# A hybrid attention trunk step on one core: a tile's rows ahead of due weight loads on SyncE, and one more mixer A head transposed on TensorE

## The chip, the cores and the metric
One core of a Trainium2 chip runs one program. The metric is the device time in microseconds (us) of one execution; the time before is the median of three runs. TensorE, VectorE (DVE), ScalarE (ACT), GpSimd (POOL) and SyncE (SP) run their own instruction streams and meet at semaphores. SP computes nothing here: it waits and issues DMAs.

## What is computed
The kernel is one layer of a diffusion trunk in float32, on 128 context tokens and 512 latent tokens (5 tiles of 128 tokens) of width 2048:

```
h = rms_norm(x) * g * (1 + scale) + shift       # scale, shift, gate = silu(cond) @ w_ada + b_ada
z = h @ w_in                                    # 2048 -> 6656 columns, the larger product
mixer A, 8 heads:  p = softmax(q1 k1) - lam * softmax(q2 k2);  o = rms_norm(p @ v) * silu(gate)
mixer B, 8 heads over 2 key heads: p = softmax(q k);           o = (p @ v) * silu(gate)
y = rms_norm(x + gate * (concat(o) @ w_out))
```

The context tile (tile 0) attends to its own 128 keys. Each latent tile (tiles 1 to 4) attends to 512 latent and 256 cached keys, 768 in all. Rotary positions, the key and value states and the cached context are part of it and are not touched here.

## The kernel before, in words
The large products are cut into 17 iterations (`it`) of 512 output columns: `it` 0 is the keys and values of mixer B, 1 to 4 are mixer B's query and gate columns (kind "G", two heads each), 5 to 12 are mixer A's heads (kind "D", one head each), 13 to 16 are the output projection. Each has 16 steps (`s`), one for each 128 rows of the weights. A step multiplies one 128x512 weight slice with the five token tiles, each as three matmuls (L775 to L777) on operands that were split into a high and a low part. `q` counts steps: q = 16 it + s from `it` 2 on. (The first two iterations are cut into pieces that take turns.)

The attention of group `a = it - 1` is laid between the products of iteration `it`, by a table of steps (`STEPS`, `STEPS_D`). For tile t, "S" is the scores, "T" the transposition of the probabilities and "V" the product with the values. S is at steps 4, 5, 7, 9, 11 for tiles 0 to 4, T at 6, 8, 10, 12, 14, V at 7, 9, 11, 13, 15. An S piece of kind "G" claims four banks one after another, one of kind "D" three, out of a ring of three PSUM banks (`claim`, L763); V claims the next bank. A bank is free when ACT has copied it out (`scores_out`, L1199). In G, the fourth score bank is the first one again; in D, the bank of V(t=0) at step 7 is the first bank of the scores of tile 2 at the same step.

**Weights.** They come in pairs of slices (pair j holds steps 2j and 2j+1; here numbered within an iteration, so pair 5 holds steps 10 and 11). SP loads a pair with two DMAs of 256 KB (`load_w`, L639) into one of two raw buffers, after VectorE has split the pair that was there: pair j waits until slice 2j-3 is split (`w_lo_done` 2j-2). At the head of its step, ACT rounds the slice of three steps on into `w_hi` (`split_w`, L1138, `W_AHEAD = 3`), and it waits for the whole pair there; VectorE then makes `w_lo` (L1541). So slice 10 is rounded at step 7.

**Probabilities.** For every latent tile, ACT copies the scores to `s_sb`, VectorE takes the maximum (`score_max`, L1640), ACT the two exponentials (`exps`, L1239), one step after S. In D, VectorE then combines the two maps into one (`combine`, L1648, `p_ready`). Transposing is done in one of two ways. `by_blocks(a, t)` is true for latent tiles of groups 1 to 11: SP writes the rows to HBM (`p_spill`, 384 KB for a map, two maps in G, one in D), waits until they have landed, and reads them back by 32-row blocks with four DMAs (`p_pair` in G, `p_block` in D; `move_blocks`, L711); VectorE transposes 32x32 blocks (`turn_blocks`, L1664), and in G ACT and VectorE split the result again (`blocks_hi`, `blocks_lo`). Otherwise TensorE transposes six 128x128 blocks into two banks (`step_t`, L933), and ACT copies them out (`pt_his`, L1248). Before, only group 12, mixer A's last head, does that for its latent tiles.

**SP's order.** SP goes through the steps. At each q whose step before held an S by blocks (steps 6, 8, 10, 12) it first issues the pairs up to q // 2 + 3 that are not yet issued, each with its wait, and then calls `move_blocks`: wait for the exponentials (G) or `p_ready` (D), spill, wait for the landing, read the blocks. At step 6 the pairs 2 to 6 are thus issued ahead of tile 1's rows; at steps 8, 10 and 12 it is one pair each.

During iteration 12 (group 11) GpSimd also reads the first output rows back from HBM (`load_row`, L2057), ACT and VectorE split them (`row_hi`, L1313).

Of the kernel before, what the change touches and what calls it, by code (L numbers as in the profile page):

```python
# [36 lines left out]
KV_IT = 0  # L37
G_IT = 1
D_IT = G_IT + H_B // 2
OUT_IT = D_IT + H_A  # L40
# [27 lines left out]
ORDER = [(it, s) for it, k0, k1 in SEGMENTS for s in range(k0, k1)]  # L68
# [57 lines left out]

def by_blocks(a, t):

    return t > 0 and KV_IT < a < OUT_IT - 1


def group_kind(a):
    return "KV" if a == KV_IT else "G" if a < D_IT else "D"
# [6 lines left out]
def steps_at(it, s):  # L140

    out = []
    if it > OUT_IT:
        return out
    if it == KV_IT + 1:
        return [("QK", KV_IT, 0)] if s == KV_QK_STEP else []
    for kind, t in (LAST_STEPS if it == OUT_IT else STEPS_D if group_kind(it - 1) == "D" else STEPS).get(s, []):
        a = it - 1
        if kind == "O":
            a, t = a + t, 0  # L150
        if not 0 <= a < OUT_IT or (group_kind(a) == "KV" and kind != "QK"):
            continue
        if kind == "O" and group_kind(a) == "G":
            continue
        out.append((kind, a, t))
        if kind == "V" and group_kind(a) == "G":
            out.append(("GT", a, t))
    return out
# [135 lines left out]
def build(nc, x_prompt, x_sample, cache_diff_k, cache_diff_v, cache_gqa_k, cache_gqa_v, c, c_ctx, w_ada,  # L294
# [120 lines left out]
    with ExitStack() as ctx:  # L415
# [48 lines left out]
        def wait_full(eng, n):  # L464

            b, i = PLACE[n]
            eng.wait_ge(bank_full[b], i + 1)
# [42 lines left out]
        def n_step(a, t):  # L510

            return TILES * (a - 1) + t
# [34 lines left out]
        def t_parts(a, t):  # L547
# [7 lines left out]
            return [(n + 2 * c + j // 4, c, j, m, 0, True) for c in hs for j, m in ((0, 4), (4, 2))]  # L555

        TURNED = [(a, t) for a in range(OUT_IT) for t in range(TILES) if by_blocks(a, t)]

        def p_count(a, t):

            return sum(heads(of) for of, u in TURNED[:TURNED.index((a, t)) + 1] if u % 2 == t % 2)

        def turns_until(a, t):

            return sum(heads(of) for of, _ in TURNED[:TURNED.index((a, t)) + 1])
# [62 lines left out]
        def ada_place(m):  # L628

            c_ = max(c for c in range(BLOCKS) if ADA_LOAD0[c] <= m)  # L630
            return c_, m - ADA_LOAD0[c_]

        def ada_slot(m):

            c_, _ = ada_place(m)
            ks = 8 // ADA_TILES[c_]
            return ada_raw[:, m % ADA_RING, :].rearrange("p (k u n) -> p k u n", k=ks, u=2), ks

        def load_w(eng, j):  # L639
            it, s = ORDER[2 * j]  # L640
            if j >= RAW_RING:

                eng.wait_ge(w_lo_done, 2 * (j - RAW_RING) + 2)
            dst = w_raw[:, j % RAW_RING]
            landed = (raw_first if RAW_RING <= j < EARLY_PAIRS else raw_in)[j % RAW_RING]
            if D_IT <= it < OUT_IT:
                for u in range(2):
                    eng.dma_start(dst[:, u, :].rearrange("p (s c) -> p s c", s=4),
                                  wa_v[it - D_IT, :, s + u]).then_inc(landed, 16)
                return  # L650
            if it == KV_IT:
                for u in range(2):
                    eng.dma_start(dst[:, u, :], w_v[:, s + u, KB0:KB0 + NCOL]).then_inc(landed, 16)
            elif it < D_IT:
                for u, c0 in enumerate((QB0, GB0)):
                    c0 += 2 * DH * (it - G_IT)
                    eng.dma_start(dst[:, :, 2 * DH * u:2 * DH * (u + 1)],
                                  w_v[:, s:s + 2, c0:c0 + 2 * DH]).then_inc(landed, 16)
            else:
                c0 = NCOL * (it - OUT_IT)  # L660
                for u in range(2):
                    eng.dma_start(dst[:, u, :], wo_v[:, MIX[s + u], c0:c0 + NCOL]).then_inc(landed, 16)
# [16 lines left out]
        @block.sync  # L679
        def _(sp):  # L680
            def load_ada(n):

                m = n - ADA_RING
                if m >= 0:
                    c_, e = ada_place(m)
                    if e == ADA_LOADS[c_] - 1:
                        wait_full(sp, TURN[("ADA", c_)])
                    else:
                        sp.wait_ge(ada_used, m - c_ + 1)
                c_, e = ada_place(n)  # L690
                dst, ks = ada_slot(n)
                w = P * ADA_TILES[c_]
                for u in range(2):
                    c0 = D_MODEL * u + P * ADA_FIRST[c_]
                    sp.dma_start(dst[:, :, u, :], ada_p[:, ks * e:ks * (e + 1), c0:c0 + w]  # L695
                                 ).then_inc(ada_in[n % ADA_RING], 16)

            def load_x(t):
                src = x_prompt[0] if t == 0 else xs_v[:, t - 1, :]
                sp.dma_start(x_sb[:, t, :], src).then_inc(x_in[t], 16)  # L700

            for t in FIRST_TILES:
                load_x(t)
            for n in range(ADA_LOADS[0]):
                load_ada(n)
            for j, t in enumerate(LATER_TILES):
                load_w(sp, j)
                load_x(t)
            for n in range(ADA_LOADS[0], sum(ADA_LOADS)):
                load_ada(n)  # L710
            def move_blocks(a, t):  # L711

                b, n = t % 2, TURNED.index((a, t))
                if group_kind(a) == "G":
                    for c_ in range(2):
                        sp.wait_ge(exp_done, 2 * n_step(a, t) + 1 + c_)
                        sp.dma_start(p_spill[b, c_], s_sb[:, b, c_, :]).then_inc(p_out[b], 16)
                else:
                    sp.wait_ge(p_ready, n_step(a, t) + 1)
                    sp.dma_start(p_spill[b, 0], s_sb[:, b, 0, :]).then_inc(p_out[b], 16)  # L720
                if n:
                    sp.wait_ge(p_turned, turns_until(*TURNED[n - 1]))
                if (a, t) == (D_IT, 1):
                    wait_full(sp, TURN[("V", D_IT - 1, TILES - 1)])
                sp.wait_ge(p_out[b], 16 * p_count(a, t))
                for i in range(QUAD):
                    rows = slice(SUB * i, SUB * (i + 1))
                    if group_kind(a) == "G":
                        src = p_spill[b].rearrange("c (j b) (i n) -> i b (c j) n", j=QUAD, i=QUAD)[i]
                        dst = p_pair[rows, :, :, :].rearrange("b c j n -> b (c j) n")  # L730
                    else:
                        src = p_spill[b, 0].rearrange("(j b) (i n) -> i b j n", j=QUAD, i=QUAD)[i]
                        dst = p_block[rows, :, :]
                    sp.dma_start(dst, src).then_inc(p_in, 16)

            j = EARLY_PAIRS
            for q in range(OPEN, len(ORDER)):
                moves = [(a, t) for kind, a, t in steps_at(*ORDER[q - 1]) if kind == "S" and by_blocks(a, t)]
                if moves:
                    while j <= min(q // 2 + 3, len(ORDER) // 2 - 1):  # L740
                        load_w(sp, j)
                        j += 1
                for a, t in moves:
                    move_blocks(a, t)
            for j in range(j, ITS * KT // 2):
                load_w(sp, j)
            for t in range(TILES - 1):
                dst = y_prompt[0] if t == 0 else y_sample[0, P * (t - 1):P * t, :]
                sp.wait_ge(y_left, t + 1)
                sp.dma_start(dst[:, 0:Y_LEFT], y_sb[:, t, 0:Y_LEFT]).then_inc(y_out, 16)  # L750
                sp.wait_ge(y_right, t + 1)
                sp.dma_start(dst[:, Y_LEFT:], y_sb[:, t, Y_LEFT:]).then_inc(y_out, 16)
            dst = y_sample[0, P * (LAT - 1):P * LAT, :]
            sp.wait_ge(y_right, TILES)
            sp.dma_start(dst[:, 2 * NCOL:3 * NCOL], y_sb[:, TILES - 1, 2 * NCOL:3 * NCOL]).then_inc(y_out, 16)
            sp.wait_ge(y_left, TILES)
            sp.dma_start(dst[:, 0:NCOL], y_sb[:, TILES - 1, 0:NCOL]).then_inc(y_out, 16)
            sp.wait_ge(y_out, 32 * (TILES + 1))
# [1480 lines left out]
```

## Time and profile before
| what | us |
|---|---|
| median of 3 runs (lowest, highest) | 1241.37 (1240.06, 1243.22) |
| the profiled execution | 1243.36 |
| its span, first to last instruction | 1241.6 |
| TensorE matmul busy | 1187.5 (96% of the span) |
| VectorE busy | 848.7 (68%) |
| ScalarE busy | 589.0 (47%) |
| GpSimd busy | 258.6 (21%) |

The span is shorter than the execution's time, since that has a start and an end in which no instruction of the program runs. "Idle" in a row is the time in which the engine had nothing running before that instruction; behind it stands what ended it. The mean granted TensorE clock over the span is 0.996 of full speed.

### The profile page before, as it was taken

The page shows a single profiled execution, that of the slowest core. Times are in us where ns is not written, and L with a number is a line of the kernel's source. Part 1 is how long each engine was busy: PE and PEld are TensorE (multiplying, and loading weights), DVE is VectorE, ACT ScalarE, POOL GpSimd, SP SyncE. Part 2 cuts the span into 40 slices and gives each one's busy share as a digit, 9 for nine tenths or more (in the row PEclk, how much of TensorE's full clock was granted, in tenths as well). Part 3 has the DMA queues.
Part 4 walks back from the last instruction along what each step waited for, and adds up shares of the span by engine and source line. Part 5 has one row for each costly group of instructions (what it writes and reads, how often), then busy time and mean ns, then how long its engine had stood idle before and what let it go on. Part 6 is the DMA issues. An engine that isn't in the chain of part 4 may idle for free.

```text
span 1241.6 us, 16426 instructions
## 1 busy us (share of the span) xinstructions
PE 1187.5 (96%) x5891; PEld 957.4 (77%) x5891; DVE 848.7 (68%) x1270; ACT 589.0 (47%) x1236; POOL 258.6 (21%) x439
## 2 busy tenths in 40 slices
PE   5899999999999999999999999999999799999996
PEld 3455788777787778888878888888878678888785
DVE  4455488768687786767667675857667574879674
ACT  5422235635556455555555464555555655312123
POOL 1211033012030030222222322222223312210111
PEclk9999999999999999999999999999999999999999
DMA  9999232635536355343444444453435523756644
GB/s 352 371 379 358 85 111 94 195 85 175 153 103 178 107 181 163 112 146 113 136 126 121 138 134 125 123 151 96 151 113 172 172 68 110 263 180 218 187 137 177
DMA packets 172658, 203.63 MB, mean 164 GB/s; under 512 B 12080, under 2 KB 131536, under 8 KB 171808
## 3 DMA queue, kind: packets, MB, share of 16 engines
q1 hardware_dynamic: 158704, 156.80, 39.9%
q0 software_dynamic: 13424, 45.20, 11.2%
q8 instruction: 47, 0.77, 0.3%
q10 hardware_dynamic: 448, 0.57, 0.1%
q14 instruction: 35, 0.29, 0.1%
HBM read 167.77 MB, written 34.75 MB: 163 GB/s over the span
## 4 chain that ended last, share of the span: by engine, by line
PE 81%; DMA 5%; DVE 4%; SPq 3%; ACT 3%; issue 3%; POOL 1%; DVEq 0%; ACTq 0%; POOLq 0%
PE z_ps L775 22%; PE z_ps L777 22%; PE z_ps L776 22%; PE ring L959 4%; SPq L695 2%; PE ring L866 2%; PE ring L963 2%; PE ring L801 2%; PE ring L900 2%; PE ring L899 2%; DMA p_pair<-p_spill 1%; DMA p_spill<-s_sb 1%; ACT s_sb L1245 1%; DMA ada_raw<-in_w_ada_dram 1%; PE ring L966 1%
## 5 line engine op out<-in xcount | busy, mean ns | idle before, releaser
L775 PE MATMUL z_ps<-w_hi,xt_hi 128*128 128x512 f32 x1350 | 544.4, 403 | 3.4 <-issue 1.1
L777 PE MATMUL z_ps<-w_hi,xt_lo 128*128 128x512 f32 x1350 | 527.7, 391 | 0.0
L776 PE MATMUL z_ps<-w_lo,xt_hi 128*128 128x512 f32 x1350 | 527.2, 391 | 0.0
L1082 ACT ACTIVATE w_hi<-w_raw 128x512 fp32r<-128x512 f32 x270 | 169.5, 629 | 340.2 <-PE z_ps L777 315.1
L775 PEld LDWEIGHTS z_ps<-w_hi,xt_hi 128*128 128x128 f32 x1350 | 254.4, 188 | 73.8 <-issue 27.2
L777 PEld LDWEIGHTS z_ps<-w_hi,xt_lo 128*128 128x128 f32 x1350 | 253.7, 188 | 54.8
L1544 DVE TENSOR_TENSOR w_lo<-w_raw,w_hi 128x512 fp32r<-128x512 f32 x270 | 195.9, 729 | 144.2 <-ACT w_hi L1082 143.4
L776 PEld LDWEIGHTS z_ps<-w_lo,xt_hi 128*128 128x128 f32 x1350 | 254.7, 189 | 43.4
L1645 DVE TENSOR_REDUCE small<-s_sb 128x2 f32<-128x1536 f32 (+1 forms) x60 | 88.0, 1467 | 22.2 <-ACT s_sb L1082 22.2
L1245 ACT ACTIVATE s_sb<-s_sb,small 128x768 f32<-128x768 f32 (+1 forms) x120 | 98.0, 820 | 3.0 <-DVE small L1645 2.7
L2028 POOL TENSOR_TENSOR sg<-sg,zs 128x128 f32<-128x128 f32 (+1 forms) x60 | 39.4, 656 | 266.1 <-DVE sg L1614 265.4
L1082 ACT ACTIVATE o_sum<-ring 128x128 f32<-128x128 f32 (+1 forms) x60 | 18.8, 313 | 153.5 <-PE ring L959 102.0
L1818 DVE SCALAR_TENSOR_TENSOR gate_acc<-gate_raw,cs,gate_acc 128x512 f32<-128x512 f32 x120 | 84.6, 746 | 3.1 <-DMA gate_raw<-in_w_ada_dram 0.6
L1614 DVE RECIPROCAL sg<-sg 128x128 f32<-128x128 f32 (+1 forms) x60 | 72.5, 1208 | 0.0
L1082 ACT ACTIVATE s_sb<-ring 128x512 f32<-128x512 f32 (+2 forms) x140 | 57.6, 473 | 11.8 <-PE ring L900 10.9
L959 PEld LDWEIGHTS ring<-v_f,pt_f 128*128 128x128 f32 x400 | 50.7, 193 | 15.1 <-issue 12.6
L959 PE MATMUL ring<-v_f,pt_f 128*128 128x128 f32 x400 | 52.2, 278 | 9.5 <-issue 6.5
L1082 ACT ACTIVATE s_sb<-ring,stat 128x512 f32<-128x512 f32 (+1 forms) x72 | 37.7, 554 | 20.2 <-PE ring L777 19.9
L899 PE MATMUL ring<-k_hi,q_hi 128*128 128x256 f32 (+2 forms) x144 | 45.0, 325 | 0.0
L963 PE MATMUL ring<-pt,v_hl 128*128 128x512 f32 x100 | 36.4, 401 | 8.8 <-issue 8.8
L900 PE MATMUL ring<-k_hi,q_lo 128*128 128x256 f32 (+2 forms) x144 | 44.0, 329 | 0.0
L1671 DVE STREAM_TRANSPOSE pt_f<-p_block 128x768 f32<-128x768 f32 x28 | 27.3, 976 | 23.3 <-DMA p_block<-p_spill 23.3
(200 smaller groups left out, 1302.0 us busy)
## 6 DMA issues: line engine op xcount, KB each, us to landing
w_raw<-in_w_in_dram SPq DMA_DIRECT2D x188, 256.0 KB, 3.2
ada_raw<-in_w_ada_dram SPq DMA_DIRECT2D x64, 512.0 KB, 11.7
p_spill<-s_sb SPq DMA_DIRECT2D x60, 384.0 KB, 3.6
w_raw<-in_w_out_dram SPq DMA_DIRECT2D x64, 256.0 KB, 3.7
p_pair<-p_spill SPq DMA_DIRECT2D x64, 192.0 KB, 3.6
gate_raw<-in_w_ada_dram POOLq DMA_DIRECT2D x12, 1024.0 KB, 7.8
p_block<-p_spill SPq DMA_DIRECT2D x112, 96.0 KB, 2.2
w_raw<-in_w_in_dram POOLq DMA_DIRECT2D x20, 256.0 KB, 6.3
```

Source lines behind the costliest of these rows:

```text
L775: pe.matmul(out, hi_l, hi_r, start=start, stop=False)
L776: pe.matmul(out, hi_l, lo_r, start=False, stop=False)
L777: return pe.matmul(out, lo_l, hi_r, start=False, stop=stop)
L899: pe.matmul(out, q_hi[c_][:, q0:q0 + P], keys, start=start, stop=False, skip_group_check=True)
L900: ins = pe.matmul(out, q_lo[c_][:, q0:q0 + P], keys, start=False, stop=True, skip_group_check=True)
L959: ins = pe.matmul(bank[:, 0:DH], pt_f[:, keys], v_f[:, vt, :], start=(j == 0), stop=last)
L1082: return act.activation(out, in_, ACT.Copy, **kw)
L1245: act.activation(row, row, ACT.Exp, bias=nmax[:, t, c_:c_ + 1], accum_out=den[:, t, c_:c_ + 1]).then_inc(exp_done, 1)
L1544: dve.tensor_tensor(lo, w_raw[:, kg // 2 % RAW_RING, kg % 2, :], hi.bitcast(F32), ALU.subtract).then_inc(w_lo_done, 1)
L1614: dve.reciprocal(sg[:, t, 0:w], sg[:, t, 0:w]).then_inc(g_inv, 1)
L1645: dve.tensor_reduce(nmax[:, t, :], s_sb[:, t % 2, :, 0:(NKEY if t else P)], AX_X, ALU.max, negate=True).then_inc(max_ready, 1)
L1818: ins = dve.scalar_tensor_tensor(acc[:, r, :], src, weight, acc[:, r, :], ALU.mult, ALU.add)
```

## The change
Two edits. `by_blocks` is now false for group 11 too, so the latent tiles of mixer A's last two heads are transposed on TensorE. And `move_blocks` is cut in two: `move_rows` waits for the rows and spills them, `move_blocks` waits for the landing and reads the blocks. At a step with moves SP now issues the pairs up to (q + 3) // 2, then the rows, then the pairs up to q // 2 + 3, then the block reads. At step 6 that puts pairs 2 to 4 ahead of tile 1's rows and pairs 5 and 6 behind them; at steps 8, 10 and 12 the first part is empty and the one pair goes behind the rows.

```diff
 def by_blocks(a, t):
-    return t > 0 and KV_IT < a < OUT_IT - 1
+    return t > 0 and KV_IT < a < OUT_IT - 2
...
-            def move_blocks(a, t):
-                b, n = t % 2, TURNED.index((a, t))
+            def move_rows(a, t):
+                b = t % 2
                 if group_kind(a) == "G":
                     for c_ in range(2):
                         sp.wait_ge(exp_done, 2 * n_step(a, t) + 1 + c_)
                         sp.dma_start(p_spill[b, c_], s_sb[:, b, c_, :]).then_inc(p_out[b], 16)
                 else:
                     sp.wait_ge(p_ready, n_step(a, t) + 1)
                     sp.dma_start(p_spill[b, 0], s_sb[:, b, 0, :]).then_inc(p_out[b], 16)
+
+            def move_blocks(a, t):
+                b, n = t % 2, TURNED.index((a, t))
                 if n:
                     sp.wait_ge(p_turned, turns_until(*TURNED[n - 1]))
...
                 moves = [(a, t) for kind, a, t in steps_at(*ORDER[q - 1]) if kind == "S" and by_blocks(a, t)]
+                if moves:
+                    while j <= min((q + 3) // 2, len(ORDER) // 2 - 1):
+                        load_w(sp, j)
+                        j += 1
+                for a, t in moves:
+                    move_rows(a, t)
                 if moves:
                     while j <= min(q // 2 + 3, len(ORDER) // 2 - 1):
                         load_w(sp, j)
                         j += 1
                 for a, t in moves:
                     move_blocks(a, t)
```

## Rows read from the trace of the kernel before
**Rows 1.** The page, part 1: busy us (share), instructions.
```profile
PE 1187.5 (96%) x5891; PEld 957.4 (77%) x5891; DVE 848.7 (68%) x1270; ACT 589.0 (47%) x1236; POOL 258.6 (21%) x439
```
**Rows 2.** Waits of TensorE, whole span: us in total, times, longest.
```profile
PE ring L963 <- issue: 8.8, 8, 2.5
PE ring L959 <- issue: 6.5, 4, 3.5
...
PE ring L775 <- ACT s_sb L1082: 2.5, 4, 0.9
```
**Rows 3.** Chain that ended last, 200 to 230 us: start, us, what.
```profile
210.20 1.96 ACT s_sb L1245 x4
...
212.24 4.15 DMA p_spill<-s_sb
```
**Rows 4.** TensorE's timeline, G group 1, idle before in brackets: tile 2's fourth score bank, tile 1's V.
```profile
215.76 0.28 PE L775 MATMUL ring<-k_hi,q_hi 128*128 128x256 f32 x1
...
228.28 0.47 PE L963 MATMUL ring<-pt,v_hl 128*128 128x512 f32 x1 [0.67 <-issue]
```
**Rows 5.** TensorE's timeline, G group 1: tile 4's V.
```profile
260.58 0.47 PE L963 MATMUL ring<-pt,v_hl 128*128 128x512 f32 x1 [2.46 <-issue]
```
**Rows 6.** SyncE's timeline, G group 1, tile 4: start, us, issues.
```profile
244.07 0.91 SPq L657 DMA_DIRECT2D w_raw<-in_w_in_dram  x2
245.03 0.94 SPq L717 DMA_DIRECT2D p_spill<-s_sb  x2
249.85 1.80 SPq L734 DMA_DIRECT2D p_pair<-p_spill  x4
```
**Rows 7.** DMA issues at 526.6 and 523.5 us: KB each, median us to landing.
```profile
p_spill<-s_sb SPq DMA_DIRECT2D x1, 384.0 KB, 2.3
...
w_raw<-in_w_in_dram SPq DMA_DIRECT2D x2, 256.0 KB, 3.1
```
**Rows 8.** SyncE's timeline in D group 5: pair 5, then tile 1's rows.
```profile
514.90 0.93 SPq L648 DMA_DIRECT2D w_raw<-in_w_in_dram  x2
...
526.60 0.34 SPq L720 DMA_DIRECT2D p_spill<-s_sb  x1
```
**Rows 9.** ScalarE's timeline in D group 5, step 7: slice 10's rounding.
```profile
525.73 0.63 ACT L1082 ACTIVATE w_hi<-w_raw 128x512 fp32r<-128x512 f32 x1 [0.72 <-PE z_ps L777]
```
**Rows 10.** ScalarE's timeline in G group 1, step 7.
```profile
212.24 0.63 ACT L1082 ACTIVATE w_hi<-w_raw 128x512 fp32r<-128x512 f32 x1
213.54 1.05 ACT L1082 ACTIVATE s_sb<-ring,stat 128x512 f32<-128x512 f32 x2 [0.67 <-PE ring L777]
```
**Rows 11.** TensorE's timeline in D group 5: V of tile 0.
```profile
530.27 0.38 PE L959 MATMUL ring<-v_f,pt_f 128*128 128x128 f32 x2
```
**Rows 12.** VectorE's timeline in G group 1, steps 7 and 8.
```profile
214.46 1.74 DVE L1614 RECIPROCAL sg<-sg 128x256 f32<-128x256 f32 x1
216.92 1.75 DVE L1645 TENSOR_REDUCE small<-s_sb 128x2 f32<-128x1536 f32 x1 [0.72 <-ACT s_sb L1082]
...
222.42 1.84 DVE L1671 STREAM_TRANSPOSE pt_raw<-p_pair 128x768 f32<-128x768 f32 x2 [2.03 <-DMA p_pair<-p_spill]
```
**Rows 13.** TensorE's timeline in group 12: four transposes of tile 1's probabilities.
```profile
1025.83 0.60 PE L866 MATMUL ring<-ident,s_sb 128*128 128x128 f32 x4
```
**Rows 14.** TensorE's timeline in group 11: V of tiles 2 and 4.
```profile
967.33 0.91 PE L959 MATMUL ring<-v_f,pt_f 128*128 128x128 f32 x6 [2.68 <-ACT s_sb L1082]
...
985.78 2.19 PE L959 MATMUL ring<-v_f,pt_f 128*128 128x128 f32 x12 [3.52 <-issue]
```
**Rows 15.** ScalarE's and VectorE's timelines in group 11: row operand, tile 4's blocks.
```profile
962.07 0.74 ACT L1082 ACTIVATE xt_hi<-row_st 128x640 fp32r<-128x640 f32 x1 [5.26 <-DMA row_st<-o_spill]
...
984.70 0.98 DVE L1671 STREAM_TRANSPOSE pt_f<-p_block 128x768 f32<-128x768 f32 x1 [3.65 <-DMA p_block<-p_spill]
```
**Rows 16.** Stages: stretch, us, busy us of each engine, granted clock, DMA share, GB/s.
```profile
985.00:990.00 5.00, 4.22 (x18) 3.77 (x19) 2.25 (x4) 1.37 (x4) 0.87 (x3) 0.66 0.29 105
...
1000.00:1055.00 55.00, 54.62 (x293) 46.37 (x294) 32.10 (x52) 31.84 (x74) 11.85 (x25) 1.00 0.28 91
```

## The prediction, made before the changed kernel ran
> **What bounds the kernel now.** I read the page's busy shares first. TensorE's matmuls cover 1187.5 us of the span, 96% [rows 1], so a change pays only where it shortens TensorE's stream or takes a wait out of it. Next the waits of TensorE [rows 2]: behind the opening, they are few and sit in the attention. Eight waits before V of kind G (L963) sum to 8.8 us, four before a score bank of G (L775) to 2.5, and four before V of kind D (L959) to 6.5. The chain of waits tells what lies behind those of G: the exponentials end at 212.16, the second spill (issued at 212.24) lands 4.15 us later, then come the reads and the transposition [rows 3]. V of tile 1 waits 0.67 in this group [rows 4], 2.7 over four groups, so tile 4's V holds the other 6.1 of the 8.8; its longest is 2.46 [rows 5].
>
> **The change part by part.** *Tile 4 in G, rows first.* SP issues a pair of weights in 0.91, then two spills in 0.94, and the reads start at 249.85 [rows 6]. The second spill's issue starts near 245.5, so it takes 4.3 to land, as in the chain (4.15). A spill with no pair just ahead lands in 2.3 [rows 7]. The new order thus brings the landing forward by 1.9 to 2.0, and by up to 0.4 more where the pair's issue held up the spill. The pair now goes out 0.9 after the second spill's issue began and lands 3.1 after its own issue [rows 7], while the reads are issued 2.3 after the spill and need about as long again to arrive: I charge them 0 to 0.5. Behind the blocks stand ACT and VectorE, both waiting. So 2.46 shrinks to about 0.5, and the other three, which share the 3.6 that is left of the 6.1 (1.2 each, less than what the landing gains), go. Gain 5.6; bounds 3 and 6.1.
>
> *Pair 5 in D.* This is what the change costs. In D group 5 the pair was issued at 514.90, and tile 1's rows, when VectorE had them ready, at 526.60 [rows 8]. Pair 5 now stands behind these rows. But it holds slice 10, which ACT rounds at the head of step 7, at 525.73 [rows 9]: before the rows are even ready. New times: spill issued 526.60 to 526.94, the pair's two DMAs from 526.98 (0.93 for both, the second near 527.4), landing of the second 3.1 to 3.3 after that, 530.6. ACT stands until then, 4.9 late. It rounds (0.63), then copies the first score bank of tile 2 (half of 1.05 [rows 10]): 531.85. That bank is the one that V of tile 0 claims, at 530.27 [rows 11]. With a hand-over of 0.1, V starts at 531.95: TensorE waits 1.7. Nothing covers it, as TensorE takes its instructions in order. What is queued behind ACT's wait is the copies, tile 0's output and the exponentials of tile 2; VectorE waits behind it for w_lo, GpSimd behind both. They lag TensorE by some 2 to 3 us at step 8, and are busy 47% and 68% [rows 1], so they regain it before tile 4: each V stands four steps behind its S. Below, a landing 2.4 after the pair's issue (nearly the lone spill's) gives 0.9; above, 4.15 (the landing behind other traffic) gives 2.7. I take 1.7, as the 3.1 is of the same DMA. Six D groups (5 to 10) are left with rows by blocks: 6 x 1.7 = +10.2; bounds +5 and +16. Tile 2 to 4's pairs (7, 8, 9) are wanted three steps after they go out, 10 us and more, against some 4 us of delay: nothing.
>
> *Tile 1 in G.* The same happens. The exponentials end at 212.16, the second spill goes out from 212.24, pair 5 from 212.7, and lands near 216.3; ACT wanted it at 212.24 [rows 10]. It rounds until 216.95 and frees the first score bank at 217.5; TensorE wanted that bank for tile 2's fourth part at 215.76 [rows 4]: a new wait of 1.8. In exchange tile 1's blocks come sooner. The spill lands at 214.6 instead of 216.4, but pairs 5 and 6 (1 MB) are now ahead of the reads, so the blocks are there near 221.5. VectorE is not ready for them: w_lo of slice 10 at 217.65, a reciprocal of 1.74, the maximum of 1.75 to 221.1 (it was 216.92 to 218.67), then the work that stood between the maximum and the transposes less its idle time: 222.42 - 2.03 - 218.67 = 1.7 [rows 12]. The transposes start at 222.9, 0.5 later than before, and V of tile 1 at 228.8 instead of 228.28. So the old waits (2.7 and 2.5 us in four groups) are swapped for new ones of the same size, plus 0.5 in this group, and a bit more where the old wait was shorter: I take 0.7 on average, +2.9. Bounds: -3 (VectorE gets its work in between) and +7 (nothing of the old waits goes).
>
> *Group 11 on TensorE.* Removed: the spill, four reads and a transpose on VectorE for each of four tiles. Added: 24 transposes on TensorE, two more banks and two copies on ACT for each tile. Four transposes take 0.60 with the tail of the last (about 0.27): 0.11 each [rows 13], six with the return to the product 0.8, four tiles 3.2. What goes: V of tile 4 waits 3.52 [rows 14] for blocks that land at 984.7 [rows 15]; and behind this wait the granted clock is 0.66 over 5 us [rows 16], a loss of 1.7. V of tile 2 waits 2.68 [rows 14] for a score copy that ACT makes late, since it stood 5.26 for a row operand [rows 15]. That stays, as the row's DMA does not belong to the change; but the transposes of tiles 1 and 2 (1.6) fall into this wait and cost nothing. ACT's extra copies, 1 us for each tile, are paid by what it no longer waits for that row, whose DMA shares its engines with fewer others; 0.4 may be over. Sum: -3.5 - 1.7 + 1.6 - 0.4 = -4.0. Bounds: +0.5 (the rows set the pace in this group whatever else goes) and -7.
>
> The clock is the place where the Trainium skill speaks against this edit. In this trace the stretch from 1000 to 1055, in which the last head's transposes lie, has a granted clock of 1.00 [rows 16], the 2.4 GHz level, and four transposes take 0.60 [rows 13]. The Trainium skill (TensorE: Matmul & The Clock Gate, Part 4: PE-mode transpose) says that transposes do not count as busy time for the clock, and gives about 275 ns for one in a kernel. By the Trainium skill's figure, an estimate, 24 would cost 6.6 us instead of 3.2, and the sum below would be 3.4 higher. The trace does not agree with it here.
>
> *Sum.* -5.6 + 10.2 + 2.9 - 4.0 = +3.5. On the profiled execution's 1243.4 that is 1246.9. The median of the runs shown is 2.0 lower (1241.4), and the same sum on it gives 1244.9, which I forecast. All terms come from one execution; their differences hold for the others too.
>
> **The rivals.**
> *The late pair stays hidden (faster).* If ACT's wait for pair 5 did not reach TensorE, the D groups would cost nothing, and in G the old waits of tile 1 would go as well: -5.6 - 5.2 + 0.5 - 4.0 = -14.3, 1227. For it: ACT and VectorE have idle time. Against it: V of tile 0 comes 3.7 after the spill's issue, and the pair can't be landed, rounded and one bank copied in that time unless its landing takes 1.6 or less. Half way between, a pair that costs 0.9 in each D group gives -1.3: 1240.
> *Reads stuck behind the pairs (much slower).* At tile 4 the reads now follow a pair on the same queue. If they land 1.5 later for it (I allow 0.5), V of tile 4 waits in every group: the G gain shrinks by 3, each D group adds 1, and the lag of ACT is not regained: +3.5 + 9 = 1254. It decides from a read landing over 1.5 behind what it was.
> *Group 11 gains nothing.* The row operands (5.26) set the pace, and copies on ACT come on top: 0 instead of -4.0, 1249.
> *The transposes slow TensorE's clock.* At the 0.66 of [rows 16] over the 3.2 us of transposes and as long again, 6.4 / 0.66 - 6.4 = +3.3: 1248. Against it stands the 1.00 of the last head's stretch. (The Trainium skill's section named above has transposes count for nothing with the clock.)
>
> **How the numbers follow.** The main case has 0.50 (own range 1241 to 1248.5, from the D term between 6.5 and 14), the hidden pair 0.08, the half hidden one 0.14, the stuck reads 0.12, group 11 without gain 0.13, the slow clock 0.03. A measurement tells 0.3% (3.7 us) from no change here, so slower begins at 1245.1. Slower: half of the main case, the stuck reads, group 11 and the clock, less a little for their low ends, 0.49. Same: the rest of the main case and most of the half hidden one, 0.39. Faster: 0.12. The range leaves out the fully hidden pair and most of the stuck reads: 1238 to 1251.
>
> **What would show it.** In the changed trace: in each D group ACT waits 4 to 5 us before the rounding of slice 10 (step 7) with w_raw's DMA as the releaser, and TensorE 1.5 to 2 before V of tile 0, in six places; in G the same wait of ACT, and about 1.8 before the last score bank of tile 2. G's spills land in about 2.3 instead of 4.15, and tile 4's V waits under 0.6. Group 11 has 24 more transposes, no wait of 3.5 before its last V and a clock of 1.00 there. I am wrong if TensorE has no wait at step 7, or if tile 4's waits in G stay.

## The result, and the profile after

| | us |
|---|---|
| before, median of 4 runs beside it (lowest, highest) | 1241.93 (1240.06, 1243.22) |
| after, median of 4 runs | 1266.27 (1262.65, 1267.34) |
| ratio, 95% interval | 1.0192 [1.0167, 1.0217] |
| span before, after | 1241.6, 1265.5 |
| forecast (range) | 1244.9 (1238 to 1251) |

The kernel became 24 us slower, and the forecast had said 3.5. To see where, I cut both spans at the first product of iterations 2, 6, 12 and 13, so that the first stretch holds groups 1 to 4 (G), the second groups 5 to 10 (D), the third group 11. Stages of the kernel before; the columns are the stretch, its length, busy us (instructions) of PE, PEld, DVE, ACT, POOL, the granted clock, DMA share and GB/s:

```profile
183.91:498.19 314.28, 302.99 (x1466) 250.13 (x1465) 237.00 (x311) 164.71 (x314) 49.73 (x42) 1.00 0.48 142
498.19:911.59 413.40, 410.28 (x2062) 345.23 (x2061) 281.64 (x431) 225.19 (x528) 104.94 (x205) 1.00 0.43 129
911.59:990.86 79.27, 71.64 (x362) 58.92 (x360) 52.99 (x82) 44.69 (x101) 27.09 (x51) 0.98 0.51 156
```

The same stages after:

```profile
184.43:497.57 313.14, 303.54 (x1466) 251.64 (x1465) 236.85 (x311) 164.12 (x314) 48.45 (x42) 0.99 0.50 142
497.57:941.95 444.38, 418.35 (x2063) 349.62 (x2061) 281.01 (x431) 221.09 (x528) 98.41 (x205) 0.98 0.43 120
941.95:1015.94 73.99, 72.57 (x385) 59.95 (x384) 49.68 (x78) 47.17 (x105) 26.27 (x48) 1.00 0.42 124
```

Length less TensorE's busy time is its idle time. G: -1.1. D: +31.0, of which idle 3.1 to 26.0 is +22.9 and busy +8.1, with the same matmuls (one record apart). Group 11: -5.3. The rest of the span: -0.7. Together +23.9, the difference of the spans.

TensorE's waits after (in us: total, times, longest) answer to [rows 2]; L969 is V of D, L973 V of G, L785 a product or score matmul, L1092 a copy on ACT:

```profile
PE ring L969 <- issue: 13.7, 6, 3.1
PE ring L969 <- ACT s_sb L1092: 12.3, 6, 2.1
...
PE ring L785 <- ACT s_sb L1092: 8.6, 4, 2.2
...
PE ring L973 <- issue: 1.0, 3, 0.6
```

The six of 12.3 are V of tile 0 at step 7 in D. The four of 8.6 are tile 2's fourth score bank in G. The six of 13.7 are V of tile 4 in D, one for each group. Before, there were 3.0 us (6.5 less group 11's 3.5 in [rows 2, 14]), in three of the six groups.

Group 5 after, step by step. SyncE's timeline, to be held against [rows 8]:

```profile
525.99 0.34 SPq L720 DMA_DIRECT2D p_spill<-s_sb  x1
526.37 2.30 SPq L648 DMA_DIRECT2D w_raw<-in_w_in_dram  x4
528.83 1.82 SPq L738 DMA_DIRECT2D p_block<-p_spill  x4
```

ScalarE's timeline there (against [rows 9]); the wait is in brackets:

```profile
530.51 0.63 ACT L1092 ACTIVATE w_hi<-w_raw 128x512 fp32r<-128x512 f32 x1 [6.12 <-DMA w_raw<-in_w_in_dram]
531.05 1.06 ACT L1092 ACTIVATE s_sb<-ring 128x512 f32<-128x512 f32 x2
```

VectorE's, which waits behind ScalarE for the same slice:

```profile
531.17 0.69 DVE L1554 TENSOR_TENSOR w_lo<-w_raw,w_hi 128x512 fp32r<-128x512 f32 x1 [4.35 <-ACT w_hi L1092]
531.78 0.94 DVE L1624 RECIPROCAL sg<-sg 128x128 f32<-128x128 f32 x1
532.79 1.75 DVE L1655 TENSOR_REDUCE small<-s_sb 128x2 f32<-128x1536 f32 x1
...
535.06 0.97 DVE L1681 STREAM_TRANSPOSE pt_f<-p_block 128x768 f32<-128x768 f32 x1
```

TensorE's, V of tile 0 at step 7 (against [rows 11]) and V of tile 4 at step 15:

```profile
531.77 0.46 PE L969 MATMUL ring<-v_f,pt_f 128*128 128x128 f32 x2 [1.97 <-ACT s_sb L1092]
...
567.31 0.91 PE L969 MATMUL ring<-v_f,pt_f 128*128 128x128 f32 x6 [3.04 <-issue]
```

Ahead of that last wait, VectorE waits twice for blocks, tile 3's and tile 4's:

```profile
555.43 0.98 DVE L1681 STREAM_TRANSPOSE pt_f<-p_block 128x768 f32<-128x768 f32 x1 [2.47 <-DMA p_block<-p_spill]
...
556.80 1.02 DVE L1672 SCALAR_TENSOR_TENSOR s_sb<-s_sb,small 128x768 f32<-128x768 f32 x1
...
566.23 0.98 DVE L1681 STREAM_TRANSPOSE pt_f<-p_block 128x768 f32<-128x768 f32 x1 [5.11 <-DMA p_block<-p_spill]
```

Most of the +8.1 of busy time sits behind some of the waits. TensorE's timeline in group 6:

```profile
605.59 0.46 PE L969 MATMUL ring<-v_f,pt_f 128*128 128x128 f32 x2 [2.04 <-ACT s_sb L1092]
...
607.87 0.63 PE L785 MATMUL z_ps<-w_hi,xt_hi 128*128 128x512 f32 x1
608.29 0.63 PE L786 MATMUL z_ps<-w_lo,xt_hi 128*128 128x512 f32 x1
...
610.46 0.39 PE L786 MATMUL z_ps<-w_lo,xt_hi 128*128 128x512 f32 x1
610.69 0.39 PE L787 MATMUL z_ps<-w_hi,xt_lo 128*128 128x512 f32 x1
```

From 606.6 to 610.0 the starts of equal matmuls are 0.43 apart, later 0.23: the clock went to its 1.2 GHz level after the wait and came back to 2.4. The stages around it (columns as above):

```profile
594.00:603.00 9.00, 9.00 (x44) 7.44 (x43) 4.32 (x6) 2.74 (x6) 3.06 (x6) 1.00 0.39 110
603.00:613.00 10.00, 7.96 (x32) 6.20 (x31) 7.12 (x9) 6.45 (x16) 1.06 (x3) 0.83 0.49 121
```

D has four such stretches at the lower level and no more; before it had none:

```profile
606.56:609.97 3.41, 3.41 (x9) 2.64 (x8) 3.24 (x3) 2.17 (x5) 0.92 (x2) 0.50 0.26 56
715.79:719.20 3.41, 3.41 (x11) 2.80 (x11) 0.90 (x2) 1.49 (x5) 1.54 (x4) 0.50 0.02 5
790.88:794.29 3.41, 3.41 (x14) 3.02 (x13) 1.45 (x3) 1.14 (x4) 0.62 (x2) 0.50 0.00 0
865.98:869.39 3.41, 3.41 (x12) 2.83 (x11) 1.00 (x2) 1.37 (x4) 1.34 (x4) 0.50 0.00 0
```

Each begins 0.6 to 1.2 us after a wait has ended: the first after a wait of 2.04 at step 7, the others after waits of 2.94, 3.15 and 2.30 at tile 4. The other eight of the twelve waits, the 3.04 above among them, had none behind them. Half of 4 x 3.41 is 6.8 of the 8.1. The other 1.3 is about what the profile adds for the waits themselves (an estimate): the last matmul ahead of a wait is shown with its whole 0.39, where the next would have begun after 0.23, and there are nine more waits.

In G, SyncE at tile 4 of group 1, against [rows 6]:

```profile
245.59 1.26 SPq L717 DMA_DIRECT2D p_spill<-s_sb  x2
246.89 1.07 SPq L657 DMA_DIRECT2D w_raw<-in_w_in_dram  x2
249.37 1.81 SPq L738 DMA_DIRECT2D p_pair<-p_spill  x4
```

The second spill (246.50) lands at 249.30, in 2.8 instead of 4.3, and tile 4's V no longer waits in any of the four groups.

### The profile page after: what moved, and what is told of

Same layout as the page of the kernel before. It is cut to its first block, busy times and chain, and to the rows that moved or that the text cites. A ratio compares the mean times of both kernels' runs of the same rounds, so it can differ in the third digit from the quotient of the medians.

```text
span 1265.5 us, 16454 instructions
## 1 busy us (share of the span) xinstructions
PE 1200.0 (95%) x5915; PEld 966.3 (76%) x5915; DVE 844.6 (67%) x1266; ACT 586.7 (46%) x1240; POOL 250.9 (20%) x439
## 4 chain that ended last, share of the span: by engine, by line
PE 79%; DMA 6%; DVE 5%; ACT 4%; issue 3%; SPq 2%; POOL 1%; DVEq 0%; ACTq 0%; POOLq 0%
PE z_ps L785 21%; PE z_ps L787 21%; PE z_ps L786 21%; PE ring L969 3%; DMA w_raw<-in_w_in_dram 3%; PE ring L876 2%; PE ring L811 2%; ACT s_sb L1255 2%; PE ring L973 2%; PE ring L910 1%; PE ring L909 1%; DMA row_st<-o_spill 1%; DMA ada_raw<-in_w_ada_dram 1%; SPq L695 1%; PE ring L976 1%
## 5 line engine op out<-in xcount | busy, mean ns | idle before, releaser
L785 PE MATMUL z_ps<-w_hi,xt_hi 128*128 128x512 f32 x1350 | 548.0, 406 | 2.6 <-issue 1.1
L1092 ACT ACTIVATE w_hi<-w_raw 128x512 fp32r<-128x512 f32 x270 | 169.6, 629 | 386.3 <-PE z_ps L787 302.1
L785 PEld LDWEIGHTS z_ps<-w_hi,xt_hi 128*128 128x128 f32 x1350 | 256.1, 190 | 73.1 <-issue 27.2
L2038 POOL TENSOR_TENSOR sg<-sg,zs 128x128 f32<-128x128 f32 (+1 forms) x60 | 35.7, 595 | 295.5 <-DVE sg L1624 295.5
L1092 ACT ACTIVATE o_sum<-ring 128x128 f32<-128x128 f32 (+1 forms) x60 | 18.9, 316 | 146.5 <-PE ring L969 95.5
L969 PE MATMUL ring<-v_f,pt_f 128*128 128x128 f32 x400 | 53.4, 282 | 26.0 <-issue 13.7
L969 PEld LDWEIGHTS ring<-v_f,pt_f 128*128 128x128 f32 x400 | 50.8, 195 | 33.2 <-issue 31.1
L1092 ACT ACTIVATE s_sb<-ring 128x512 f32<-128x512 f32 (+2 forms) x136 | 55.1, 476 | 3.6 <-PE ring L910 3.4
L1681 DVE STREAM_TRANSPOSE pt_f<-p_block 128x768 f32<-128x768 f32 x24 | 23.4, 976 | 41.6 <-DMA p_block<-p_spill 41.5
L1092 ACT ACTIVATE s_sb<-ring,stat 128x512 f32<-128x512 f32 (+1 forms) x72 | 37.3, 554 | 15.2 <-PE ring L787 14.9
L1972 POOL TENSOR_SCALAR small<-small 128x1 f32<-128x1 f32 x40 | 8.0, 199 | 153.9 <-ACT sq_o L1298 152.9
```

What stands on the lines that cost most here:

```text
L785: pe.matmul(out, hi_l, hi_r, start=start, stop=False)
L969: ins = pe.matmul(bank[:, 0:DH], pt_f[:, keys], v_f[:, vt, :], start=(j == 0), stop=last)
L1092: return act.activation(out, in_, ACT.Copy, **kw)
```

## The experiments

Each kernel below stands beside runs of the kernel before on one chip, but not all kernels ran on the same chip; the stretches are from one profiled execution of each. L(G), L(D) and L(11) are the lengths of the three stretches, D's waits are those of the waits view, (the bank that ACT frees late, at step 7; V of tile 4), and D's busy time is that of the stages. Each ratio is to the runs of before beside that kernel, whose medians are 1241.1 to 1243.0.

```
kernel                    median (runs)  ratio [95%]             L(G)   L(D)   L(11)  D: ACT's bank, tile 4, busy
before                    1241.9 (4)                             314.3  413.4  79.3    -     3.0   410.3
group 11 only             1234.6 (4)     0.9950 [.9932, .9967]   313.5  412.6  73.3    -     2.4   410.2
order only                1274.9 (4)     1.0273 [1.0256, 1.0290] 313.7  437.6  85.6   12.4  10.1   415.1
changed kernel            1266.3 (4)     1.0192 [1.0167, 1.0217] 313.1  444.4  74.0   12.3  13.7   418.4
pair 5 ahead              1231.6 (4)     0.9914 [.9895, .9932]   302.0  421.0  73.6    -     8.8   412.1
late pair only            1262.6 (4)     1.0170 [1.0152, 1.0188] 319.4  435.8  74.3   12.6   6.8   416.4
rows ahead in G only      1225.6 (6)     0.9858 [.9837, .9879]   303.4  413.6  73.8    -     3.3   410.3
 + D tile 4               1227.7 (5)     0.9882 [.9863, .9901]   302.3  415.7  73.8    -     5.1   410.7
 + D tiles 1 to 3         1228.7 (6)     0.9894 [.9874, .9914]   301.9  416.9  73.9    -     6.3   410.6
 + group 10 on TensorE    1227.1 (5)     0.9876 [.9857, .9894]   302.1  415.4  74.1    -     2.3   413.1
 + late pair 5, 6 behind  1245.7 (10)    1.0028 [1.0011, 1.0044] 302.2  435.8  73.3   12.8   6.6   416.5
changed + copies first    1271.8 (4)     1.0243 [1.0219, 1.0267] 315.0  447.9  73.6    1.4  25.1   421.4
late pair + copies first  1275.2 (4)     1.0276 [1.0249, 1.0303] 322.6  440.1  74.0    1.9  18.4   419.7
G only + copies first     1236.3 (6)     0.9951 [.9936, .9967]   311.7  414.2  73.6    -     4.1   410.2
```

("Order only" runs the same code in D as the changed kernel, and its D is 6.8 shorter: 3.6 of it at tile 4's waits, and 3.3 in busy time, as it has two stretches at the low clock where the changed kernel has four. So with the late pair a stage of D is reproduced only to some 7 us, where it is 412.6 to 413.6 in the three kernels that keep the order of before in D. With copies first, the waits for ACT's bank, 1.4 and 1.9, are at step 9, and those put down to tile 4 hold one or three small ones of other tiles.)

**Group 11 only**, to the kernel before:
```diff
-    return t > 0 and KV_IT < a < OUT_IT - 1
+    return t > 0 and KV_IT < a < OUT_IT - 2
```


> Only group 11's latent tiles go to TensorE; SP's order is that of the kernel before. In the changed kernel, iteration 12 takes 74.0 us from its first product to the next iteration's, against 79.3 before. Both theories below say nothing of it; if the edits add up, this kernel is 4 to 6 us faster than before (1236 to 1238) with iteration 12 at 74. If the gain in iteration 12 hangs on the other edit, it is under 2 us.

Measured: 0.9950 [0.9932, 0.9967], 1234.6, a little under the expected 1236 to 1238; group 11 is shorter by 5.9. The edit is a gain by itself.

**Order only**: the changed kernel with `OUT_IT - 1` again.

> Only SP's order is changed; group 11 is still transposed by blocks. If the edits add up: the 24.3 us of the whole change plus the 5.3 that group 11 gives, about +30 us (1271 to 1273). Group 11 now also has a late pair 5 and rows ahead, so some 2 to 6 us more are possible (up to 1278).

Measured: 1.0273, 1274.9, inside what was expected. The order carries the whole loss, and without the other edit group 11 suffers from it too: 85.6 against 79.3.

**Pair 5 ahead of tile 1's rows** (pair 6 still behind them, and one pair behind the rows at steps 8, 10 and 12):
```diff
-                    while j <= min((q + 3) // 2, len(ORDER) // 2 - 1):
+                    while j <= min((q + 4) // 2, len(ORDER) // 2 - 1):
```


> The changed kernel with one number different: pair 5 goes ahead of tile 1's rows at step 6 ((q + 4) // 2 instead of (q + 3) // 2); at steps 8, 10 and 12 the rows stay ahead. Theory (late pair): all D waits follow from slice 10 coming late; the six waits of 2.2 before V of tile 0 go, tile 4's waits in D fall from 14.7 to about 4, the slow clock behind them goes, and G gets both its gains: 1225 to 1230. Rival (reads stuck): tile 4's waits in D come from the reads behind a pair at steps 10 and 12; they stay at 12 to 15 us with part of the slow clock, and the time is about 1240 to 1246.

**Late pair only**: step 6 as in the change, steps 8, 10 and 12 as before.
```diff
-                    while j <= min((q + 3) // 2, len(ORDER) // 2 - 1):
+                    while j <= min((q + 3) // 2 if q % KT == 6 else q // 2 + 3, len(ORDER) // 2 - 1):
```


> The changed kernel with the late pair alone: pairs 5 and 6 behind tile 1's rows at step 6, but at steps 8, 10 and 12 the pair ahead of the rows as before. Theory (late pair): tile 4's waits in D stay at 10 us or more, as ACT's and VectorE's lag reaches tile 4 by itself; in G tile 4's waits (6 us) come back: 1264 to 1272. Rival (reads stuck): tile 4's waits in D fall to 4 or less; with G's 6 us back the time is 1252 to 1258.

Measured: with the pair in time, no wait at step 7 is left, and the kernel is faster than before, 0.9914 [0.9895, 0.9932]. But neither pair of expectations holds at tile 4. With the pair in time its waits are 8.8, between the theory's 4 and the rival's 12 to 15, and 1231.6 is above the theory's range; with the late pair alone they are 6.8, between the rival's 4 or less and the theory's 10 or more. Both edits reach tile 4. With "group 11 only" and the changed kernel these two make a square of D: 412.6 (neither), 421.0 (rows ahead), 435.8 (late pair), 444.4 (both). The late pair costs 23, the rows ahead 8 to 9, and the two add up to the 444.4, but not to the 437.6 of "order only": the sum is known no better than D is reproduced. TensorE's waits with the late pair alone:

```profile
PE ring L969 <- ACT s_sb L1092: 12.6, 6, 2.3
PE ring L785 <- ACT s_sb L1092: 8.6, 4, 2.4
PE ring L969 <- issue: 6.8, 4, 3.3
PE ring L973 <- issue: 5.3, 4, 2.4
```

Its +23.2 in D are 12.6 at step 7, 4.4 more at tile 4 (6.8 against 2.4) and 6.2 of busy time, with three stretches of 3.41 at the low clock (5.1). The +8.4 of the rows ahead are 6.4 at tile 4 (8.8 against 2.4) and 2.0 of busy time, with one such stretch (1.7).

**Rows ahead in G only**: pair 5 in time, D in the old order.
```diff
-                    while j <= min((q + 3) // 2, len(ORDER) // 2 - 1):
+                    while j <= min((q + 4) // 2 if group_kind(moves[0][0]) == "G" else q // 2 + 3, len(ORDER) // 2 - 1):
```


> The changed kernel, but with pair 5 ahead of tile 1's rows in G, and with the order of before at every tile in D (all due pairs ahead of the rows); group 11 on TensorE as changed. Theory (the three parts add up: G gains 12 where pair 5 is not late, D loses nothing with the old order, group 11 gains 6): groups 1 to 4 take 302, groups 5 to 10 take 413, the time is 1223 to 1225 against 1241. The rival, that G's gain has a price later (VectorE or the queues carry a lag from G into D), keeps D at 418 or more and the time at 1228 or more.

Measured: 1225.6, just above the expected range and the fastest of all; D is 413.6, so nothing is paid back later. Its waits:

```profile
PE ring L969 <- issue: 3.3, 4, 1.5
PE ring L973 <- issue: 1.9, 4, 0.7
```

On top of it, the same bound with `or moves[0][1] == 4` behind the G (tile 4 of D too), or with `or moves[0][1] < 4` (tiles 1 to 3 of D):

> As the kernel with rows ahead in G only, but in D tile 4's rows too go ahead of the one pair due at step 12; tiles 1 to 3 of D keep the order of before. With rows ahead at all tiles of D (pair 5 in time) D takes 8.4 us more. Theory (reads stuck behind a pair at tile 4 itself): the whole of it is here, D 419 to 422, and V of tile 4 waits 1.3 in the mean. Rival (the lag comes from tile 3's later turn on VectorE, in front of tile 4's combination): D stays at 413 to 415, or gets shorter, since tile 4's spill lands earlier: 1223 to 1226.

> The counterpart: as the kernel with rows ahead in G only, but in D the rows of tiles 1 to 3 go ahead of pairs (pair 5 still ahead of tile 1's rows, so never late), tile 4 keeps the order of before. Theory (reads stuck behind a pair at tile 4 itself): D 413 to 415, time 1223 to 1226. Rival (the lag comes through tile 3's turn on VectorE): D 419 to 422, time 1230 to 1233.

Measured: D +2.1 and +3.3. Neither expectation holds: each half of D pays its part, and together (421.0) they cost 2.0 more than the sum, of which the one stretch at the low clock is 1.7. The intervals of the ratios overlap with that of the kernel they build on (0.9858 [0.9837, 0.9879]), but every run of both is slower than every run of it (1226.69 and up, against 1226.58 and down), and the D waits (3.3, 5.1, 6.3, 8.8) go the same way. ACT waits for no weight slice in D in these kernels, so the pairs that go out behind the rows are not late themselves.

**Group 10 on TensorE too** (`OUT_IT - 3`):

> As the kernel with rows ahead in G only, but group 10's heads too keep their transposes on TensorE. If group 11's 6 us came from waits that only group 11 has (a row operand's DMA and blocks 3.5 late), group 10 gains nothing or loses: 24 transposes of 0.11 are 2.6 us, against waits of about 1.5 in an iteration of D: +1 to +2, 1225. If each group of D pays for its blocks as group 11 did, 3 to 5 us go: 1220.

Measured: iteration 11 takes 71.1 instead of 68.3, D +1.8. The first case held, within 2 us of its 1225 (1227.1): group 11's gain came from waits of its own.

**Copies first**: in the changed kernel, at step 7, ACT copies tile 2's scores before it rounds slice 10.
```diff
+                copies_first = G_IT < it < OUT_IT and s == 7
-                if kg < ITS * KT:
+                if kg < ITS * KT and not copies_first:
                     split_w(kg)
...
                     elif kind == "S":
                         scores_out(a, t)
+                if copies_first:
+                    split_w(kg)
```


> The changed kernel with one move on ACT: at step 7 of groups 1 to 11 it copies tile 2's score banks before it rounds slice 10, so that the wait for the late pair no longer stands ahead of the bank that V of tile 0 (D) or tile 2's fourth score bank (G) claims. The pair is as late as before, and so is w_lo of slice 10, which TensorE needs three steps later. Theory (the 2 us at step 7 are this order on ACT, and the slow clock behind them follows them): both rows of TensorE's waits at step 7 go (12.3 in D, 8.6 in G), matmul-busy time in D falls by about 4, and D is 425 to 430 against 444, G about 305: 1240 to 1245. Rival (VectorE and ACT are as late as before against TensorE, so the time comes back at tile 4's V): its six waits in D grow from 13.7 to 20 or more, D 437 or more, 1255 or more.

> The same move on ACT in the kernel that has the late pair alone (rows ahead at step 6, the order of before at 8, 10 and 12): D was 435.8 there and 412.6 with the pair in time. Theory: the step 7 waits (about 12) and their slow clock go, D 418 to 422, 1240 or so (G has its tile 4 waits). Rival (the lag comes back at tile 4): D 428 or more, 1250.

> The move on ACT on top of the fastest kernel so far (rows ahead in G only, pair 5 in time; 1225.6), where no wait stands at step 7. Theory: without a late pair the order on ACT is worth nothing: 1224 to 1227, D 413 to 415. Were it worth something by itself (copies 0.6 sooner for VectorE's maximum), 1222; were slice 10's rounding now on TensorE's path, 1229 or more.

Measured: in the first two kernels the theory fell and the rival held, with 1271.8 and 1275.2 far above 1255 and 1250. In the third D stayed as the theory had it (414.2), but the time was 1236.3: the last of its three cases, the rounding on TensorE's path. V's waits in the changed kernel with copies first:

```profile
PE ring L969 <- issue: 25.1, 9, 5.0
...
PE ring L969 <- ACT s_sb L1092: 1.4, 2, 1.2
```

Step 7's 12.3 is gone (the 1.4 is at step 9), tile 4's 13.7 has become 25: the same sum, 26, to within 0.5. The third kernel, which has no late pair, shows how. VectorE's timeline in G group 1 with copies first:

```profile
217.55 0.69 DVE L1557 TENSOR_TENSOR w_lo<-w_raw,w_hi 128x512 fp32r<-128x512 f32 x1 [3.35 <-ACT w_hi L1092]
218.16 1.75 DVE L1627 RECIPROCAL sg<-sg 128x256 f32<-128x256 f32 x1
219.82 1.70 DVE L1658 TENSOR_REDUCE small<-s_sb 128x2 f32<-128x1536 f32 x1
```

And with ACT's old order, in the kernel it builds on:

```profile
214.14 0.63 DVE L1554 TENSOR_TENSOR w_lo<-w_raw,w_hi 128x512 fp32r<-128x512 f32 x1
214.68 1.74 DVE L1624 RECIPROCAL sg<-sg 128x256 f32<-128x256 f32 x1
217.15 1.75 DVE L1655 TENSOR_REDUCE small<-s_sb 128x2 f32<-128x1536 f32 x1 [0.72 <-ACT s_sb L1092]
```

VectorE makes `w_lo` ahead of tile 2's maximum. Whatever delays the rounding of slice 10 delays the maximum (2.7 here), the exponentials and the score copies of tile 3, and TensorE then waits 1.35 for a bank (5.4 in four groups, of G's +8.3).

**Pair 6 behind the reads**: on "rows ahead in G only", step 6 of D is rows, pair 5, reads; pair 6 goes at step 8, with pair 7, ahead of tile 2's rows.
```diff
-                    while j <= min((q + 4) // 2 if group_kind(moves[0][0]) == "G" else q // 2 + 3, len(ORDER) // 2 - 1):
+                    while j <= min((q + 4) // 2 if group_kind(moves[0][0]) == "G" else (q + 3) // 2 if q % KT == 6 else q // 2 + 3, len(ORDER) // 2 - 1):
...
-                    while j <= min(q // 2 + 3, len(ORDER) // 2 - 1):
+                    while j <= min((q + 4) // 2 if group_kind(moves[0][0]) == "D" and q % KT == 6 else q // 2 + 3, len(ORDER) // 2 - 1):
```


> The kernel with rows ahead in G only (1225.6, D 413.6), but at step 6 of D: tile 1's rows, then pair 5 (so late as in the changed kernel), then tile 1's reads; pair 6 goes behind them, at step 8 ahead of tile 2's rows, still in time. So half as many bytes stand between tile 1's rows and its reads as with the late pair before. The last read of tile 1 landed 13.5 us after step 6's first product with the late pair and 10.9 with the pair in time. Theory A (ACT's wait for pair 5 is what costs, the reads' place adds little): six waits of 2 at step 7 stay and D is 433 to 438, as with the late pair alone (435.8); the time is 1245 to 1250. Theory B (the other half of the cost is tile 1's reads behind 1 MB of weights, which make VectorE late up to tile 4): the step 7 waits stay, but the last read lands near 12.5, tile 4's V waits go back to 3 us in all, and D is 424 to 430, 1236 to 1241.

Measured: D is 435.8, the same as with both pairs between rows and reads, though tile 1's last block lands 1.7 sooner. Tile 1's reads are hidden (VectorE's transposition at 535.06 above had no wait). Theory A held (1245.7). ACT waits for weights six times in D, at step 7 alone, so pair 6 is in time, and what costs is slice 10, which comes late.

Where each D group stands, from SyncE's timelines: the issue of a tile's rows and the landing of its last block, us after the first product of the step (6, 8, 10, 12 for tiles 1 to 4), mean of six groups:

```
kernel                     rows of tile 1  2     3     4     last block of tile 1  tile 4
group 11 only                     4.69  4.86  4.78  4.66          10.91        12.30
rows ahead in G only              4.69  4.84  4.77  4.63          10.88        12.43
 + D tile 4                       4.69  4.94  4.83  4.60          10.99        12.91
 + D tiles 1 to 3                 4.69  5.54  5.49  5.26          11.59        13.13
pair 5 ahead                      4.69  5.53  5.64  5.36          11.59        13.54
 + late pair 5, 6 behind          4.69  6.10  5.75  5.27          11.69        12.96
late pair only                    4.69  6.13  5.74  5.49          13.39        13.07
order only                        4.69  6.13  5.80  5.57          13.36        13.75
changed kernel                    4.69  6.13  6.23  6.14          13.58        14.36
changed + copies first            4.69  8.54  8.37  8.22          13.72        16.39
```

The last column goes with tile 4's waits nearly one for one. Against "group 11 only" the last block lands 0.8 later with the late pair alone, 1.2 with the rows ahead alone and 2.1 with both, and TensorE waits 0.7, 1.1 and 1.9 more in each group (4.4, 6.4 and 11.3 in six). Rows ahead at tiles 1 to 3 alone delay tile 4's rows, which keep their old order, by 0.6: a delay is handed on from tile to tile.

## Why the prediction was wrong

**The sequence was right, up to V of tile 0.** Forecast for D group 5: rows at 526.60, rounding of slice 10 at 530.6, V at 531.95 after a wait of 1.7. Measured: 525.99, 530.51, 531.77, 1.97. The pair landed 3.6 after its second issue (526.85 to 530.49), not 3.1. Six such waits are 12.3, against +10.2.

**The step that failed** is the sentence that ACT and VectorE "lag TensorE by some 2 to 3 us at step 8, and are busy 47% and 68%, so they regain it before tile 4". They do not, or only in part. TensorE's waits at step 7 let the others catch up by 2 us, and the rows of tiles 2, 3 and 4 still go out later after their steps begin than in the order of before: by 1.3, 1.0 and 0.8 with the late pair alone, by 0.7, 0.9 and 0.7 with the rows ahead alone, by 1.3, 1.5 and 1.5 with both. So the sentence fails for the late pair, and its neighbour fails too, that pairs 7, 8 and 9 behind the rows of tiles 2 to 4 cost nothing: the pairs are in time, but the reads that now stand behind them land later. A share of busy time says little here: between S and V of a tile lies a chain in which one engine waits for the next and for two DMAs, and VectorE serves two tiles and the weights in one order. In the changed kernel its wait of 2.47 for tile 3's blocks stands ahead of tile 4's combination. And tile 4 had next to no slack to give: its V already waited in three of the six groups, 3.0 in all, and of that row I used only group 11's part. The four steps between S and V were a count of steps, not a measured reserve. Tile 4's V waits went from 3.0 to 13.7: +10.7 where I had 0. By the kernels with one of the two parts, about 4.4 of it come from the late pair and 6.4 from the rows ahead.

**The busy time behind the waits** is the second term that is missing, +8.1, of which 6.8 are the four stretches at the low clock. I charged the clock in group 11, from [rows 16], and not in D, where the change makes twelve waits: six at step 7, forecast, and six at tile 4, unforeseen. Three of the four stretches stand behind tile 4's. 12.3 + 10.7 + 8.1 = 31.1, D's +31.0.

**The rival "Reads stuck behind the pairs"** had the mechanism of the missing lag, at 1254 and a chance of 0.12, but the wrong trigger. A read that stands behind a pair costs what I allowed: tile 4's last block lands 0.5 later with the rows ahead at tile 4 alone (12.43 to 12.91), and D grew by 2.1. In the changed kernel it lands 2.1 later (12.30 to 14.36), which passes the rival's own mark of 1.5, but 1.5 of that is the rows going out later and only the rest the reads. The rival added 1 us for each D group; tile 4's waits alone grew by 1.8, and the rival, too, left out the clock.

**In G** the parts were near. Tile 4: forecast -5.6, its four waits (6.1) went. Tile 1: forecast +2.9; the new waits are 8.6 (forecast 7.2), the old 5.2 went but for 1.0, and matmuls took 0.55 more: +4.95. The sum is the -1.1 of the stage; I had -2.7.

**Group 11**: forecast -4.0, measured -5.3 here. The transposes cost what was said: busy time grew by 0.9 net, with the clock at 1.00 instead of 0.98. TensorE's stage has only one wait of 1.3 left, which was there before; V of tile 2's 2.68 went too, though I kept it. ACT's longest wait for a row operand fell from 5.26 [rows 15] to 2.94 (2.7 with group 11's edit alone); why the row comes sooner was not tested:

```profile
990.80 0.74 ACT L1092 ACTIVATE xt_hi<-row_st 128x640 fp32r<-128x640 f32 x1 [2.94 <-DMA row_st<-o_spill]
```

By the Trainium skill (TensorE: Matmul & The Clock Gate, Part 4: PE-mode transpose) the 24 would cost 6.6 us, an estimate from its 275 ns, and would not count as busy time for the clock. The trace again does not agree: four take 0.60, here in the middle of a stage at 1.00:

```profile
977.75 0.60 PE L876 MATMUL ring<-ident,s_sb 128*128 128x128 f32 x4
```

**What stays open.** Why some D groups with the late pair catch up and others don't was not settled: rows of tile 4 go out between 4.56 and 6.90 after their step in the changed kernel. Nor is it known why the clock fell after some waits and not after longer ones, nor how large its part would be without the waits at tile 4.

## What to carry to other kernels

A transfer moved back in a queue is to be held against its earliest reader, and then against everything that stands behind that reader on its engine and on the engines that wait for it: freeing one of them (copies first) only moved the wait to the next place. Before "it is regained" is written, look for the last consumer's wait in the trace of before. Where it is already above zero there is no slack. Here it was so in three of six groups, and nearly every us by which tile 4's blocks came later was a us of TensorE's waiting, plus what the clock lost behind it. Here pair 5 one place earlier, and the old order kept in D, give 0.9858 [0.9837, 0.9879] in place of 1.0192 [1.0167, 1.0217].

## What the runs showed of the hardware

- A wait of TensorE of 2.04 was followed by 3.41 us at the 1.2 GHz level, and one of 3.04 by none. Over D, twelve waits of 26.0 us in sum had four such stretches behind them, which cost 6.8.
- A spill of 384 KB landed in 2.3 with nothing issued right ahead of it or behind it ([rows 7]), in 2.8 with a pair of weights issued right behind it, and in 4.15 to 4.3 with one ahead ([rows 3, 6]; second of two spills). So weights that go out behind a spill slowed it too, by a quarter of what those ahead of it did: 0.5 against 1.9.
